# One decoder step on one Trainium2 core: last mean by token, combine in five banks, table clears moved behind the cached values, first projection read one item ahead

## The reference

```python
# layer 0
z = gelu(rms(x) @ a_w_in); u, v = split(z)          # 1024 -> 2 x 1024
v = layernorm(v)                                     # over 1024 channels
x = x + (u * (W_s v + b)) @ a_w_out                  # W_s mixes tokens inside a chunk of 128
x = x + (silu(n @ w_gate) * (n @ w_up)) @ w_down     # n = rms(x)
# shared keys and values, then layer 1
kv = rms(x) @ w_kv                                   # cached pages are read beside it
x = x + attention(rms(x), kv, cached pages, cached window) @ b_w_out
top = top2(rms(x) @ w_router + b)
x = x + sum_m gate[m] * expert[top[m]](rms(x))       # SwiGLU 1024 -> 2816 -> 1024
y = x * rsqrt(mean(x * x) + eps) * norm_final        # the end
```

## Time and profile before

| | us |
|---|---|
| median of 3 runs | 1326.03 (1325.71 to 1331.93) |
| the profiled execution, whole | 1325.86 |
| its span, first to last instruction | 1324.3 |
| PE busy | 1248.7 (94%) |
| PE's weight loads busy | 1063.9 (80%) |
| DVE busy | 1042.1 (79%) |
| ACT busy | 927.7 (70%) |
| POOL busy | 76.4 (6%) |

### The profile page before, as it was taken

One profiled execution on the slowest core, in us unless ns is written; L12 is line 12 of the kernel. 1 busy time (PEld: TensorE's weight loads), 2 busy tenths in 40 slices (PEclk: granted clock), 3 DMA queues, 4 the chain that ended last, 5 costly groups with the idle time before them and its releaser, 6 DMA issues.

```text
span 1324.3 us, 21438 instructions
## 1 busy us (share of the span) xinstructions
PE 1248.7 (94%) x7272; PEld 1063.9 (80%) x7272; DVE 1042.1 (79%) x1463; ACT 927.7 (70%) x1378; POOL 76.4 (6%) x77
## 2 busy tenths in 40 slices
PE   6889999999996879999999999999999999999996
PEld 6879999999964668788788888888888888887874
DVE  6767666567523965898998998998998998989985
ACT  5555444456462895787987987987888888878863
POOL 1000000004210000200000000000000000003400
PEclk9999999999996889899999999999999999999998
DMA  8374455557589108699998998998998998998930
GB/s 342 129 252 172 183 191 192 191 191 254 160 318 418 61 4 347 266 423 393 357 416 333 388 413 322 406 406 319 413 402 324 415 392 333 416 380 326 410 133 33
DMA packets 59711, 391.50 MB, mean 296 GB/s; under 512 B 6686, under 2 KB 12962, under 8 KB 21186
## 3 DMA queue, kind: packets, MB, share of 16 engines
q1 hardware_dynamic: 51010, 354.29, 68.0%
q0 software_dynamic: 8640, 36.40, 7.4%
HBM read 367.41 MB, written 27.45 MB: 298 GB/s over the span
## 4 chain that ended last, share of the span: by engine, by line
PE 73%; DVE 10%; ACT 7%; issue 5%; SPq 3%; DMA 2%; DVEq 0%; ACTq 0%
PE bank L1838 16%; PE bank L1840 16%; PE bank L1839 16%; PE bank L1469 7%; PE bank L1470 7%; PE bank L1471 7%; DVE w_lo L1351 3%; ACT arena L756 2%; SPq L429 2%; DMA win_v_past<-in_win_v 2%; DVE d_lo L969 1%; PE bank L1823 1%; ACT slc_v L763 1%; ACT d_hi L604 1%; ACT w_hi L831 1%
## 5 line engine op out<-in xcount | busy, mean ns | idle before, releaser
L1351 DVE TENSOR_TENSOR w_lo<-raw,w_hi 128x1024 fp32r<-128x1024 f32 x528 | 622.7, 1218 | 36.0 <-ACT w_hi L831 18.4
L831 ACT CAST w_hi<-raw 128x1024 fp32r<-128x1024 f32 x528 | 543.2, 1056 | 93.3 <-PE bank L1840 92.3
L1838 PE MATMUL bank<-w_hi,xg_hi 128*128 128x512 f32 x704 | 275.0, 391 | 1.5 <-DVE w_lo L1351 1.5
L1840 PE MATMUL bank<-w_hi,xg_lo 128*128 128x512 f32 x704 | 274.4, 390 | 0.0
L1839 PE MATMUL bank<-w_lo,xg_hi 128*128 128x512 f32 x704 | 274.0, 389 | 0.0
L969 DVE TENSOR_TENSOR d_lo<-ring,d_hi 128x1024 fp32r<-128x1024 f32 x120 | 146.0, 1223 | 92.4 <-ACT d_hi L604 92.3
L1469 PE MATMUL bank<-hA_hi,d_hi 128*128 128x264 f32 x640 | 185.9, 291 | 18.4 <-DVE hA_lo L959 9.1
L1470 PE MATMUL bank<-hA_lo,d_hi 128*128 128x264 f32 x640 | 183.2, 286 | 0.0
L1471 PE MATMUL bank<-hA_hi,d_lo 128*128 128x264 f32 x640 | 182.9, 286 | 0.0
L604 ACT CAST d_hi<-ring 128x1024 fp32r<-128x1024 f32 x120 | 124.8, 1043 | 66.9 <-PE bank L1471 60.0
L1838 PEld LDWEIGHTS bank<-w_hi,xg_hi 128*128 128x128 f32 x704 | 132.1, 188 | 29.3 <-DVE w_lo L1351 2.2
(11 more groups left out here) (311 smaller groups left out, 1485.1 us busy)
## 6 DMA issues: line engine op xcount, KB each, us to landing
raw<-in_moe SPq DMA_DIRECT2D x264, 1024.0 KB, 6.7
ring<-in_wd SPq DMA_DIRECT2D x29, 2048.0 KB, 8.4
out_rows<-zeros POOLq DMA_DIRECT2D x1, 6656.0 KB, 60.3
slot_rows<-zeros POOLq DMA_DIRECT2D x1, 6144.0 KB, 30.3
out_rows<-yrow POOLq DMA_DIRECT2D x8, 512.0 KB, 7.0
xs<-slot_rows POOLq DMA_DIRECT2D x7, 512.0 KB, 3.6
arena<-in_cmp_pages POOLq DMA_DIRECT2D x16, 128.0 KB, 3.3
X2v<-in_cmp_pages POOLq DMA_DIRECT2D x16, 128.0 KB, 2.6
```

The source lines that it names most:

```text
L831: nc.scalar.copy(w_hi[:, i % NSPLIT, :], raw[:, u % NRAW, ITEM * (i % 2):ITEM * (i % 2) + ITEM])\
L1351: V.tensor_tensor(w_lo[:, i % NSPLIT, :], raw[:, (i // 2) % NRAW, ITEM * (i % 2):ITEM * (i % 2) + ITEM], w_hi[:, i % NSPLIT, :].bitcast(F3 ...
L1838: T.matmul(out, lhs_hi, hi, start=first, stop=False)
L1840: return T.matmul(out, lhs_lo, hi, start=False, stop=last)
```

## The change

Four places are edited.

1. First stage: ACT and DVE split one item further ahead. On ACT the cast of an item stands ahead of the gelu that it followed. On DVE the split stands behind the scaling of a result and ahead of the sum of squares, and the work of the layer norm is interleaved in another way with the scalings of `u`.
2. POOL waits for all cached values before it issues the clears of the two tables.
3. Last block: the weighting of rows read back moves one slice later; `add_back` moves from slices 9 and 10 (four each) to slice 10 (four), the place ahead of `down(9)` (two) and the place ahead of `down(10)` (two). `add_combined` of chunks 4 to 7 moves behind the block.
4. End: ACT copies the left half of the result as soon as the left bank is done, DVE copies the right half. ACT then loads the table of the root. The combine uses five banks. The mean is taken by token: for each chunk three small products (squares as the stationary matrix, one column of 1/1024 as the moving one) are accumulated in `B[2]`. Root and reciprocal work on columns of tokens, and three products with the identity spread the result over all partitions into `MISC`, which the last scaling reads. `y` is stored in four pieces.

```diff
+        LAST_BANKS = [T0, T1, B[0], B[1], STAT, T0, T1, B[0]]
 # SP
-            for half in range(2):
-                sp.wait_ge(h_ready, 28 + 4 * half)
-                sp.dma_start(y_out[:, 4 * half:4 * half + 4, :], hB[:, 4 * half:4 * half + 4, :]).then_inc(y_stored, 16)
+            for q in range(4):
+                sp.wait_ge(h_ready, 26 + 2 * q)
+                sp.dma_start(y_out[:, 2 * q:2 * q + 2, :], hB[:, 2 * q:2 * q + 2, :]).then_inc(y_stored, 16)
 # POOL
             pool.wait_ge(zeros_ready, 1)
+            pool.wait_ge(past_v_in, 16 * (NS * PAGES + 1))
 # ACT
             for c in range(KC):
-                round_to("vu", c)
+                round_to("vu", c + 1)
                 act.wait_ge(v_scaled, c + 1)
...
-                round_to("vu", KC + c)
+                round_to("vu", KC + c + 1)
...
-                    if ends and 6 <= f < 9:
-                        back_weighted(f - 6)
+                    if ends and 7 <= f < 10:
+                        back_weighted(f - 7)
...
-            rows_out(last + 1)
-
+            act.wait_ge(left_done, 1)
+            act.wait_ge(yrow_free, last + 2)
+            nc.scalar.copy(yrow[:, 0:512], B[2][:, :]).then_inc(left_ready, 1)
+            root_table()
...
-            std(7, 0)
+            act.wait_ge(mean_done, 7)
+            nc.scalar.activation(tok_rstd[:, 0:2], B[2][:, 0:2], ACT.Sqrt, bias=vector("eps")[:, 0:1])
+            nc.scalar.activation(tok_rstd[0:NS, 2:3], B[2][0:NS, 2:3], ACT.Sqrt, bias=vector("eps")[0:NS, 0:1]).then_inc(tok_std, 1)
 # DVE
             for k in range(KC):
-                rest_to("vu", k)
                 scaled(vT[:, k, :], "vu", k, v_scaled)
+                rest_to("vu", k + 1)
                 if k:
                     add_up(vT, k - 1, v_ready, k)
...
-                    if ends and f >= 9:
-                        for c in range(4 * f - 36, 4 * f - 32):
+                    if ends and f == FT - 1:
+                        for c in range(4):
                             add_combined(0, c)
...
-            for c in range(KC + 1):
-                if c < KC:
-                    add_combined(1, c)
-                if c:
-                    add_up(sq_last, c - 1, sq_ready, 32 + c)
-            inv_std()
-            normed(late("final"))
+            for c in range(4, KC):
+                add_combined(0, c)
+            dve.wait_ge(item_used, last * ITEMS + ITEMS + NSPLIT)
+            dve.wait_ge(yrow_free, last + 2)
+            V.tensor_copy(yrow[:, 512:1024], B[3][:, :]).then_inc(right_ready, 1)
+            for c in range(KC):
+                add_combined(1, c)
+            dve.wait_ge(tok_std, 2)
+            V.reciprocal(tok_rstd[:, 0:2], tok_rstd[:, 0:2]).then_inc(tok_scale, 1)
+            V.reciprocal(tok_rstd[0:NS, 2:3], tok_rstd[0:NS, 2:3]).then_inc(tok_scale, 1)
+            dve.wait_ge(rstd_spread, 1)
+            for k in range(KC):
+                V.scalar_tensor_tensor(hB[:, k, :], x[:, k, :], late("final")[:, k:k + 1], MISC[:, 0:NT], ALU.mult, ALU.mult)\
+                    .then_inc(h_ready, 1)
 # PE
+            def last_mean(k):
+                pe.wait_ge(sq_ready, 32 + k + 1)
+                for t, (a, z) in enumerate(spans):
+                    i = T.matmul(B[2][0:z - a, t:t + 1], sq_last[:, k, a:z], mean[:, 0:1], start=(k == 0 and t == 0), stop=(k == KC - 1 and t == 2),
+                                 skip_group_check=True)
...
-                    if ends and f >= 9:
-                        for c in range(4 * f - 36, 4 * f - 32):
+                    if ends and f == FT - 1:
+                        for c in range(4):
                             add_back(c)
...
                 turn_hidden(FT - 1)
+                if ends:
+                    add_back(4)
+                    add_back(5)
                 down(FT - 2)
+                if ends:
+                    add_back(6)
+                    add_back(7)
                 down(FT - 1)
...
             for c in range(KC):
                 combine(c)
-
-            mean_of()
+                if c >= 4:
+                    last_mean(c - 4)
+            for k in range(4, KC):
+                last_mean(k)
+            pe.wait_ge(tok_scale, 4)
+            for t, (a, z) in enumerate(spans):
+                r = z - a
+                i = T.matmul(MISC[:, a:z], tok_rstd[0:r, t:t + 1].to_broadcast([r, P]), ident[0:r, 0:r], start=True, stop=True)
+            i.then_inc(rstd_spread, 1)
```

More of the change, by code:

```diff
@@ L380, in build @@
         comb_done, comb_added = sem("comb_done"), sem("comb_added")
+        left_done, left_ready, right_ready = sem("left_done"), sem("left_ready"), sem("right_ready")
+        rstd_spread = sem("rstd_spread")
         v_stored, kv_stored, past_stored, y_stored = sem("v_stored"), sem("kv_stored"), sem("past_stored"), sem("y_stored")
@@ L945, in add_up @@
                 nsum[0] += 1
-            def normed(weight):
-                for k in range(KC):
-                    V.scalar_tensor_tensor(hB[:, k, :], x[:, k, :], weight[:, k:k + 1], rstd[:, :], ALU.mult, ALU.mult)\
-                        .then_inc(h_ready, 1)
             nrest = [0, 0]
@@ L996, in _ @@
             add_up(vT, KC - 1, v_ready, KC)
-            rest_to("vu", 8)
+            u_scale(0)
+            rest_to("vu", 9)
             dve.wait_ge(mean_done, 2)
@@ L1001, in _ @@
                 V.tensor_tensor(vT[:, k, :], vT[:, k, :], mu[:, :], ALU.subtract).then_inc(ctr_ready, 1)
-            u_scale(0)
-            u_scale(1)
-            for k in range(KC):
-                if k == 4:
-                    u_scale(2)
-                rest_to("vu", 9 + k // 4)
+                if k == 3:
+                    u_scale(1)
+                    rest_to("vu", 10)
+            for k in range(4):
+                add_up(hB, k, csq_ready, k + 1)
+            u_scale(2)
+            rest_to("vu", 11)
+            for k in range(4, KC):
                 add_up(hB, k, csq_ready, k + 1)
             u_scale(3)
-            rest_to("vu", 11)
+            rest_to("vu", 12)
             inv_std(ln_rstd)
             for k in range(KC):
-                if k == 5:
-                    rest_to("vu", 12)
+                if k == 3:
                     u_scale(4)
+                    rest_to("vu", 13)
                 V.scalar_tensor_tensor(vT[:, k, :], vT[:, k, :], vector("lng")[:, k:k + 1], ln_rstd[:, :], ALU.mult, ALU.mult)\
                     .then_inc(ln_scaled, 1)
-            rest_to("vu", 13)
-            u_scale(5)
-            u_scale(6)
-            u_scale(7)
+            for c in range(5, KC):
+                u_scale(c)
+                rest_to("vu", 9 + c)
             for i in range(0, 6, 2):
@@ L1362, in add_combined @@
                 dve.wait_ge(comb_done, n * KC + c + 1)
-                V.tensor_tensor(x[:, c, :], x[:, c, :], (STAT, MISC)[c % 2][:, 0:NT], ALU.add).then_inc(comb_added, 1)
+                bank = LAST_BANKS[c] if n else (STAT, MISC)[c % 2]
+                V.tensor_tensor(x[:, c, :], x[:, c, :], bank[:, 0:NT], ALU.add).then_inc(comb_added, 1)
             def back_summed(t):
@@ L1408, in expert_block @@
                         V.tensor_copy(GwT[:, :], MISC[:, 0:NT]).then_inc(gwT_ready, 1)
-                    if ends and 6 <= f < 9:
-                        back_summed(f - 6)
-                    if ends and f >= 9:
-                        for c in range(4 * f - 36, 4 * f - 32):
+                    if ends and 7 <= f < 10:
+                        back_summed(f - 7)
+                    if ends and f == FT - 1:
+                        for c in range(4):
                             add_combined(0, c)
@@ L1809, in combine @@
                 if c == 0:
-                    pe.wait_ge(yrow_ready, 2 * last + 4)
-                pe.wait_ge(comb_added, KC + c - 1)
-                T.matmul((STAT, MISC)[c % 2][:, 0:NT], yrow[:, c * P:(c + 1) * P], GwT[:, :], start=True, stop=True)\
-                    .then_inc(comb_done, 1)
+                    pe.wait_ge(left_ready, 1)
+                if c == 4:
+                    pe.wait_ge(right_ready, 1)
+                    pe.wait_ge(comb_added, KC)
+                if c >= 5:
+                    pe.wait_ge(comb_added, KC + c - 4)
+                T.matmul(LAST_BANKS[c][:, 0:NT], yrow[:, c * P:(c + 1) * P], GwT[:, :], start=True, stop=True)\
+                    .then_inc(comb_done, 1)
+            def last_mean(k):
[3 more added lines that the diff above has]
+                                 skip_group_check=True)
+                if k == KC - 1:
+                    i.then_inc(mean_done, 1)
             pe.wait_ge(blk_ready, 1)
@@ L1848, in down @@
                                         slice(512 * half, 512 * half + 512), slot, f == 0 and j == 0, f == FT - 1 and j == 1)
+                            if ends and f == FT - 1 and j == 1 and half == 0:
+                                i.then_inc(left_done, 1)
                         i.then_inc(item_used, 1)
```

3 lines of the change are left out of this document (1 added, 2 removed).

## The result

The changed kernel takes 1318.55 us (median of 10 runs, 1309.38 to 1320.49) against 1327.17 for the kernel before (10 runs). The ratio is 0.9923, 95% interval 0.9906 to 0.9940: faster by 0.8%, where 1.4% was forecast, and outside the range of 1301.5 to 1315. The profiled execution took 1318.52 us with a span of 1316.9; before it was 1325.86.

A forecast was written before the change was run, and what follows sets the result against it. PE was taken as the bound, busy 94% of the span, with time to gain only where it waits or ends a serial chain. Terms -7.0 - 6.5 - 4.2 - 1.1 = -18.8 gave 1307.0 us, range 1301.5 to 1315.

The forecast's parts named there:

- the first stage's term, -7.0: First stage: splitting one item further ahead removes PE's waits for splits; -7.0 us, bounds -4 to -8.5.
- second mean: First stage, layer norm: PE's wait for this mean grows from 1.6 to 2.5 us; both means together +0.3.
- turning: First stage, behind product 15: PE turns v, and DVE's first copy stands behind more work; +1.4 us.
- a bound of 1.3 us: First stage: the 2.5 us wait could cost what the earlier 3.08 us wait cost in clock, +1.3.
- Rival 1: First stage gives only -3, as the second mean's wait sinks the clock or PE waits at the turning; 1311 us, 15%.
- Both recorded signs of a clock of 0.5: Signs listed as showing the forecast wrong: granted clock of 0.5 in the first stage or behind the last block.
- Rival 4: First and next stage: clock stays down after the second mean through twelve products, 35 us at half rate; 1342 us, 2%.
- Clears: Cached values: window values land before DVE's copy, so PE starts at 413.72 and not 420.28; -6.5 us, range -5.5 to -7.5.
- Rival 3: Cached values: window values still land late because SP's own 6 MB hold them; PE starts at 420 as before; 1313.5 us, 7%.
- Last block: Last block: moving add_back gives -6.74 at slice 10's turning, of which 2.5 come back; -4.2 us, bounds -3 to -4.8.
- End: Program's end: faster root, reciprocal and spread -0.8, smaller last store -0.3, mean 0; -1.1 us, bounds -2 and +5.7.
- Rival 2: End: the mean's small products run at half clock or slower than in the router, 6.5 us more; 1313.5 us, 9%.

The follow-up runs named there:

- the execution with the clock up: Profiled run of the changed kernel with four unread products added ahead of the second turning of v alone; 1310.38 us, ratio 0.9855 to the kernel before.
- the mean filled: The changed kernel with six unread products of 264 columns added ahead of the layer norm's second mean alone; 1314.01 us, ratio 0.9884 to the kernel before.
- the reordered kernel: The changed kernel with squares 4 to 7 ahead of the third gelu, sums ahead of the third scaling, last split left out; 1315.11 us, ratio 0.9903.
- the best version: The changed kernel with its first stage reordered and unread products, cut to the waits, ahead of five PE waits; 1303.84 us, ratio 0.9824 to the kernel before.

## Why the prediction was right and where it failed

**The failed step is the first stage's term, -7.0.** Its waits were right in the main: splits -6.4 of -6.9, second mean 2.88 (2.5), turning +1.7 (+1.4); only the mean before them stayed at 1.27 and was to fall to 0.4. What it mis-sized is what these waits do to the clock. It priced the second mean at +0.3 and the turning at +1.4, as time in which PE stands, and took a fall of the clock for a bound of 1.3 us, since in the kernel before it had cost about that. Set against the execution with the clock up, the changed kernel reaches the turning 3.0 us later (68.54 against 65.53), needs 6.5 us more from there to the mixing's end, and loses 1.3 more behind it, where 18 products run at 0.22 us and not at 0.12, less what PE waits there anyway. That is the whole of the 10.8 us by which the term was off; 0.25 of it lies ahead of the first fall.

**Why the same fall was cheap before.** After the 3.08 us wait came 264-column products in a dense row, and the clock was back 2.8 us later. Behind the second mean, where the same products follow, it took some 6, and 3.9 in the run with the first stage's edit alone. After the turning come small products of 128 and 8 columns, and it was back only 4 us after the next dense products had begun; with the mean filled and in the reordered kernel the clock likewise stayed at 0.50 over the whole mixing, and with the first stage's edit alone it was back before it. So small products behind a wait went with a long fall in three profiles of four. The bound was taken from one fall in the old place, with what followed there.

**Rival 1 named both places**, with 15%, but its price of 4 us has no row of its own; measured it is 10.8, and 1311 became 1318.5. That time lies in the band of 1317 to 1320 which the forecast gave, with 3%, to two rivals together; it is there by one rival at nearly three times its price, so the band fits by luck. Both recorded signs of a clock of 0.5 came, in the first stage and behind the last block, and the mixing started at 76.28 and not between 72 and 73.5. Its counterargument, that a wait of 1.6 us at 55 us left the clock at full, says nothing about 2.5. Rival 4, the clock down through twelve products, did not come.

**Clears: right**, in size and in the releaser. Rival 3 did not come: with SP's two tiles right behind, the window values landed in 8.5 us, the time of any such load. One detail was not right: SP issued the 16 value pages in 17.16 us, 1.07 each, and not in the 1.4 that the forecast held fixed. It had taken that from the key pages, which took 1.40 each in both kernels, almost all of them before the clears were issued; what sets that pace stays open. PE was waiting for DVE, so it gave nothing.

**Last block: right** to 0.1 us, with the wait ahead of the seventh `add_back` 0.38 for 0.6.

**End: -0.5 for -1.1.** Left copy, combines and small products came out to 0.1 us, and the first activation stands 1.30 us after the table load began, as in the earlier trace rows. The spread had been taken from an `add_back` at full clock, 0.53, and two things were wrong with that. An `add_back` is three records and the spread six: the earlier trace rows shows six in 1.06, for two `add_back`. A group of the mixing is three products of the spread's size and took 0.96 at full clock, which is an estimate for the spread. And the clock was 0.50, so it took 1.74, close to the mixing's 1.67. So the first scaling starts 11.5 us behind the last expert product, as before (11.35), and the 0.5 come from the smaller last store: 2.5 us from the last scaling to the end, where it was 3.1. Rival 2 had the right idea one step too early: what falls is the clock behind the one-column products. One unread product ahead of the spread in the best version did not change it (still 1.74), and three cost more than they saved.

**What stays open.** Not settled is why the clock fell after 2.88 us in one kernel and held after 2.87 in another with the same order up to that point, nor what keeps it down afterwards: the turnings are transposes and the mixing ordinary small products, with short waits between, and no run separates these. Each experiment has one profile, so how often the clock takes either course is known only from mean clocks and times. Of the changed kernel's ten runs nine lie between 1316.91 and 1320.49 and one at 1309.38, with the highest mean clock, 0.980 against 0.972 to 0.975. That fits one execution without the falls, but it has no profile.

## What to carry to other kernels

Price a longer wait of PE twice: the time it stands, and what runs behind it at half clock, taken from the instructions that follow in the new place and not from where such a fall was seen before. Where a wait like these of 2.4 to 3.1 us stands ahead of small products, shorten it or lay unread products ahead of it, counted by their measured length. A gain ahead of a transfer that does not move with it (the window values landed between 419 and 423 us in the three profiles with the clears in their old place, whenever the first stage ended) is worth little until that transfer moves: the order of edits decides what each seems to bring. And a gain at one stage is followed to the end: here 7.6 us at the gate product came with 2.2 us lost in attention. Before a small product is priced from a row, count the records of both.

## What the runs showed of the hardware

- Ten unread products at two waits took 9.3 us off a kernel of 1318 us (7.3 by the ratios). The clock can be held up by work without use.
- Once at 0.50, the clock stayed there for 18 us while PE was busy 17.29 of 18.00 us, most of it with small products (74 to 92 us).
- The clock also fell where PE hardly waited: behind 3.27 us of one-column products it went from 1.00 (up to 1308.7 us) to 0.50 (from 1309.3), with a wait of 0.73 us between; in the best version it fell at the same place with PE busy throughout (0.79 over 1293 to 1294).
- The same wait (2.36 to 2.43 us at the turning) was followed by 0.50 over the whole mixing in two profiles and by full clock at the mixing in a third.
- With 12.8 MB of zeros under way on POOL's queue SP took 1.43 us to issue a value page and the page 13.3 us to land; without them 1.07 and 2.1. The key pages took 1.40 to issue in the changed kernel too, with no zeros under way, so these are not the only thing that slows an issue.
